# Output-gate projection of the mLSTM mixer in 16 pieces between the steps of its head loop, gate by tanh

## The reference

```python
def mlstm_mixer(h, w_in, conv_w, conv_b, gate_b, head_gain, w_out):
    z = h @ w_in                        # columns: q and k (raw), v, o, gates
    ...
    h_fwd = mlstm_chunkwise(q, k, v, g[0, 0], log_sigmoid(g[0, 1]))      # 8 heads, chunks of 128 tokens
    h_bwd = flip(mlstm_chunkwise(flip(q), flip(k), flip(v), ...))
    hs = (h_fwd + h_bwd).transpose(0, 2, 1, 3)
    hs = rms_norm(hs) * head_gain       # over the 128 columns of each head; eps = 1e-6
    out = jax.nn.sigmoid(o).reshape(...) * hs
    return out.reshape(B, S, 1024) @ w_out
```

## Time and profile before

| what | value |
|---|---|
| three runs | 2610.43, 2621.83, 2626.52 us; median 2621.83 |
| profiled execution | 2625.2 us; its span, from first to last instruction, 2623.4 us |
| mean granted TensorE clock over the span | 0.961 |
| TensorE busy | 2515.0 us, 96% of the span |
| VectorE, ScalarE, GpSimd busy | 1237.9, 907.2, 66.6 us (47%, 35%, 3%) |
| instructions | 30460 |

### The profile page before, as it was taken

The page is one execution under the profiler, slowest core; times in us unless marked ns, Lnnn a source line. Parts: engine busy times, 40 slices in busy tenths (PEclk is TensorE's granted clock), DMA queues, the critical chain, the costliest instruction groups (busy, mean ns, idle before and its releaser), DMA issues.

```text
span 2623.4 us, 30460 instructions
## 1 busy us (share of the span) xinstructions
PE 2515.0 (96%) x12342; PEld 2076.9 (79%) x12342; DVE 1237.9 (47%) x1476; ACT 907.2 (35%) x1221; POOL 66.6 (3%) x80
## 2 busy tenths in 40 slices
PE   7989999999998999999999999999988999999998
PEld 6657888888996678888878888799856977788886
DVE  6678533357624553332254441546585623544423
ACT  3453333213424333332243331334444434433311
POOL 0300000000002000000000000000000000000000
PEclk9999999998996699999999999999988999999999
DMA  8135522472222022222222222231100330222221
GB/s 339 52 119 199 186 89 96 176 272 80 99 69 95 21 80 98 96 96 96 92 84 96 96 96 96 79 111 65 65 17 17 121 120 33 80 96 96 96 96 64
DMA packets 40407, 267.36 MB, mean 102 GB/s; under 512 B 4378, under 2 KB 5658, under 8 KB 9218
## 3 DMA queue, kind: packets, MB, share of 16 engines
q1 hardware_dynamic: 31248, 219.87, 23.4%
q0 software_dynamic: 5696, 40.37, 4.0%
q10 hardware_dynamic: 3378, 5.91, 0.7%
HBM read 263.90 MB, written 2.24 MB: 101 GB/s over the span
## 4 chain that ended last, share of the span: by engine, by line
PE 85%; DVE 8%; ACT 4%; issue 1%; DMA 1%; ACTq 0%; SPq 0%; DVEq 0%
PE bank L222 24%; PE bank L223 24%; PE bank L224 24%; PE bank L1852 2%; ACT w_hi L205 1%; DVE w_lo L209 1%; PE bank L1850 1%; PE bank L325 1%; DMA work<-stream 1%; PE bank L2132 1%; PE bank L2215 1%; PE bank L253 1%; PE bank L254 1%; PE bank L259 1%; DVE work L449 1%
## 5 line engine op out<-in xcount | busy, mean ns | idle before, releaser
L222 PE MATMUL bank<-h_hi,w_hi 128*128 128x512 f32 x1880 | 740.9, 394 | 7.4 <-DVE h_lo L564 2.3
L224 PE MATMUL bank<-h_hi,w_lo 128*128 128x512 f32 x1880 | 735.1, 391 | 0.0
L223 PE MATMUL bank<-h_lo,w_hi 128*128 128x512 f32 x1880 | 734.7, 391 | 0.0
L209 DVE TENSOR_TENSOR w_lo<-raw,w_hi 128x2048 fp32r<-128x2048 f32 x192 | 440.9, 2296 | 602.0 <-ACT w_hi L205 602.0
L205 ACT ACTIVATE w_hi<-raw 128x2048 fp32r<-128x2048 f32 x192 | 366.4, 1908 | 425.9 <-PE bank L224 417.2
L222 PEld LDWEIGHTS bank<-h_hi,w_hi 128*128 128x128 f32 x1880 | 355.0, 189 | 87.7 <-issue 8.4
L224 PEld LDWEIGHTS bank<-h_hi,w_lo 128*128 128x128 f32 x1880 | 354.8, 189 | 75.2
L223 PEld LDWEIGHTS bank<-h_lo,w_hi 128*128 128x128 f32 x1880 | 355.2, 189 | 72.7 <-issue 0.5
L222 PE MATMUL bank<-g_hi,w_hi 128*128 (+1 forms) x704 | 279.1, 396 | 0.0
L223 PE MATMUL bank<-g_lo,w_hi 128*128 (+1 forms) x704 | 279.1, 396 | 0.0
L224 PE MATMUL bank<-g_hi,w_lo 128*128 (+1 forms) x704 | 279.1, 396 | 0.0
(11 more groups left out here) (290 smaller groups left out, 2772.9 us busy)
## 6 DMA issues: line engine op xcount, KB each, us to landing
raw<-stream SPq DMA_DIRECT2D x192, 1024.0 KB, 4.8
work<-stream POOLq DMA_DIRECT2D x19, 1024.0 KB, 6.9
h_plain<-stream POOLq DMA_DIRECT2D x16, 1024.0 KB, 5.4
work<-stream SPq DMA_DIRECT2D x13, 1024.0 KB, 12.5
work<-mlstm_rows ACTq DMA_DIRECT2D x8, 512.0 KB, 4.7
x<-xT SPq DMA_DIRECT2D x1, 2048.0 KB, 9.3
outT<-work SPq DMA_DIRECT2D x8, 256.0 KB, 2.3
work<-mlstm_rows ACTq DMA_DIRECT2D x8, 192.0 KB
```

The source lines that it names most:

```text
L209: nc.vector.tensor_tensor(w_lo[:, slot(m), :], raw[:, slot(m), :], w_hi[:, slot(m), :], ALU.subtract).then_inc(lo_split, 1)
L222: nc.tensor.matmul(out, stationary[0], moving[0], start=first, stop=False)
L223: nc.tensor.matmul(out, stationary[0], moving[1], start=False, stop=False)
L224: return nc.tensor.matmul(out, stationary[1], moving[0], start=False, stop=last)
```

## The change

1. Units 9 to 12 leave the row of units. Right after unit 8 TensorE makes all eight carried states.
2. The work of units 9 to 12 is cut into 16 pieces (`piece`), each one block of 128 tokens of one unit: 8 x 3 = 24 products of 256 columns. Piece r is put ahead of the sums of step r-1, two of them ahead of step 0. The pieces write banks 0 and 1, two pieces to a bank.
3. With banks 2 and 3 alone left, `score` makes one head at a time, at every odd step: 4 products (8 instructions) on one half of the rows.
4. ScalarE evacuates two pieces at a time with `tanh(x / 2)` (`take_gate`, 8 instructions of 128 x 512) in place of four sigmoids of 128 x 1024, and no longer changes its table between exponentials and gate. `gate_rows` becomes `(tanh + 1) * rows`, which is twice the sigmoid's product; the factor of two is taken back in the roots (`scale=4/group`, `bias=4 eps`).
5. The split of units 11 to 14 of the stream (counted from this stage's first) moves into the head loop: high parts behind every second `take_gate`, low parts on VectorE at steps 4, 8, 12 and 16.
6. `scale_keys` and the first transfer of queries are made one or several units earlier; buffers in SBUF are moved so that these can live beside each other.

Cut to its core:

```diff
@@ scalar
-                for u in range(13):
+                for u in range(9):
-                    if u == 12:
-                        self.exps(act, st, 0)
-                        self.exps(act, st, 1)
-                        act.wait_ge(self.s_moved, 48)
-                        self.load_queries(act, 1)
-                        nc.scalar.activation(self.o[:, :, c:c + 256], two_banks(m), ACT.Sigmoid).then_inc(self.s_evac, 1)
+                self.exps(act, st, 0)
+                for i in range(8):
+                    self.copy_state(act, i)
+                self.exps(act, st, 1)
+                act.wait_ge(self.s_moved, 48)
+                self.load_queries(act, 1)
                 for q in range(2, 2 * self.H):
+                    if d == 0:
+                        self.take_gate(act, h - 1)
                     self.exps(act, st, q)
...
+            def take_gate(self, act, g):
+                m, c = self.m0 + 9 + g // 2, 256 * (g // 2)
+                if g % 2:
+                    act.wait_ge(unit_used, m + 1)
+                else:
+                    act.wait_ge(self.s_pe_prep, 15 + g // 2)
+                nc.scalar.activation(self.o[:, 2 * (g % 2):2 * (g % 2) + 2, c:c + 256],
+                                     bank[:, g % 2, :].rearrange("p (t n) -> p t n", t=2), ACT.Tanh,
+                                     scale=0.5).then_inc(self.s_evac, 1)
+                if g % 2:
+                    split_next_hi(act, m)
@@ vector
-                    if u == 8:
+                    if u == 7:
                         self.scale_keys(dve)
-                    if q >= 4 and q % 2 == 0:
-                        self.tail.gate_rows(dve, q // 2 - 2)
-                self.tail.gate_rows(dve, self.H - 1)
+                    if q % 4 == 0 and q:
+                        split_next_lo(dve, self.m0 + 8 + q // 4)
+                    if q >= 6 and q % 4 in (2, 3):
+                        self.gate(dve, 2 * (q // 4) - 4 + q % 4)
+                for h in (self.H - 2, self.H - 1):
+                    self.gate(dve, h)
                 self.tail.vector(dve, st)
@@ tensor
-                    if u in (9, 10):
-                        pe.wait_ge(self.s_keys, 12)
-                        pe.wait_ge(self.s_evac, 9)
-                        for p in range(4):
-                            self.add_state(pe, u - 9, p)
-                pe.wait_ge(self.s_copied, 8)
+                pe.wait_ge(self.s_keys, 12)
+                pe.wait_ge(self.s_evac, 9)
+                for d in range(2):
+                    for p in range(4):
+                        self.add_state(pe, d, p)
+                pieces = 0
                 self.score(pe, 0)
                 for q in range(2 * self.H):
-                    if q % 4 == 2 and q < 14:
-                        self.score(pe, (q + 2) // 4)
+                    if q % 2 and q < 15:
+                        self.score(pe, (q + 1) // 2)
+                    while pieces < min(q + 2, 16):
+                        self.piece(pe, pieces)
+                        pieces += 1
+                    if q == 0:
+                        pe.wait_ge(self.s_copied, 8)
                     self.sum_values(pe, q)
...
+            def piece(self, pe, r):
+                m, t, g = self.m0 + 9 + r // 4, r % 4, r // 2
+                wh, wl = unit_cols(m)
+                if t == 0:
+                    pe.wait_ge(lo_split, m + 1)
+                if r % 2 == 0 and g >= 2:
+                    pe.wait_ge(self.s_evac, 8 + g)
+                c = slice(t * P, t * P + P)
+                for k in range(KC):
+                    last = three_passes(bank[:, g % 2, (r % 2) * 256:(r % 2) * 256 + 256], (h_hi[:, k, c], h_lo[:, k, c]),
+                                        (wh[:, k, :], wl[:, k, :]), k == 0, k == KC - 1)
```

More of the change, by code:

```diff
@@ L59 @@
           ("hg_gnorm", 4), ("sb_gnorm", 4), ("gate_b_i", 1), ("gate_b_f", 1), ("eps", 1), ("zero", 1),
-          ("one", 1), ("half", 1)]
+          ("one", 1), ("half", 1), ("eps4", 1)]
 PCOL = {}
@@ L908, in take_roots @@
                 act.wait_ge(self.sq, self.groups)
-                nc.scalar.activation(self.roots, self.sums, ACT.Sqrt, bias=eps, scale=1.0 / self.group).then_inc(
-                    self.root, 1)
+                four = 4.0 if self.gate_tanh else 1.0
+                nc.scalar.activation(self.roots, self.sums, ACT.Sqrt, bias=col("eps4") if self.gate_tanh else eps,
+                                     scale=four / self.group).then_inc(self.root, 1)
             def gate_rows(self, dve, b):
@@ L914, in gate_rows @@
                 c = slice(b * P, b * P + P)
+                if self.gate_tanh:
+                    nc.vector.scalar_tensor_tensor(self.rows[:, :, c], self.gate[:, :, c], 1.0, self.rows[:, :, c],
+                                                   ALU.add, ALU.mult).then_inc(self.gated, 1)
+                    return
                 nc.vector.tensor_tensor(self.rows[:, :, c], self.rows[:, :, c], self.gate[:, :, c],
@@ L1451, in program @@
             rows_out = area(21056, S + 3 * P)
-            e, se = area(16448, 2, S), area(17472, 2, S)
-            qs = [area(18496 + 768 * a, 2, 3 * P) for a in range(2)]
+            e = [area(19520, S), area(16448, S)]
+            se = area(18496, 2, S)
+            qs = [area(a, 2, 3 * P) for a in (3328, 16960, 17728, 16960)]
             c = [area(20032 + 387 * a, 3, P + 1) for a in range(8)]
@@ L1678, in vector, with gate @@
                         self.scale_queries(dve, (q + 2) // 4)
[L1679 to L1681 removed]
+                    if q % 4 == 0 and q:
[4 more added lines that the diff above has]
+                    self.gate(dve, h)
                 self.tail.vector(dve, st)
+            def gate(self, dve, h):
+                dve.wait_ge(self.s_evac, 9 + 2 * (h // 2) + 2)
+                self.tail.gate_rows(dve, h)
             def factors(self, st):
@@ L1820, in add_state, with score @@
                 last.then_inc(self.s_pe_prep, 1)
[L1822 to L1829, removed]
+            def piece(self, pe, r):
[9 more added lines that the diff above has]
+                                        (wh[:, k, :], wl[:, k, :]), k == 0, k == KC - 1)
+                if t == 1:
+                    last.then_inc(self.s_pe_prep, 1)
+                if t == 3:
+                    last.then_inc(unit_used, 1)
+            def score(self, pe, h):
+                if h >= 2:
+                    pe.wait_ge(self.s_se, 2 * h - 2)
+                half = slice(64 * (h % 2), 64 * (h % 2) + 64)
                 for a in range(TB):
                     t = slice(a * P, a * P + P)
[L1832 to L1835, removed]
+                    last = nc.tensor.matmul(bank[:, 2 + h % 2, t], self.qk[half, 4 + h // 2, t], self.qk[half, h // 2, t],
+                                            start=True, stop=True)
                 last.then_inc(self.s_scored, 1)
@@ L2671, in build_params @@
             columns(i["final_norm_2"]), columns(i["hg_lb_raw_2"]), columns(i["hg_gnorm_2"]), columns(i["sb_gnorm_2"]),
-            gb, np.full((P, 1), EPS, f), np.zeros((P, 1), f), np.ones((P, 1), f), np.full((P, 1), 0.5, f)]
+            gb, np.full((P, 1), EPS, f), np.zeros((P, 1), f), np.ones((P, 1), f), np.full((P, 1), 0.5, f),
+            np.full((P, 1), 4 * EPS, f)]
     out = np.ascontiguousarray(np.concatenate(cols, axis=1))
```

31 lines of the change are left out of this document (14 added, 17 removed).

## The result

The changed kernel took 2579.85 us (median of four, 2578.01 to 2582.02) against 2623.98 us for the kernel before in the same comparison. The ratio is 0.9842, with a 95% interval of 0.9807 to 0.9878: 1.6% faster. The forecast was 2611.7 us with a range of 2588 to 2632, so the result lies outside it. It is 5.8 us from the first rival, in which the clock holds (2585.6 us).

What follows compares the result with a forecast made beforehand. TensorE at half clock was taken to bound the head loop. The loop was to end 11.3 us earlier (full-clock gain 37.4, less 26 for falls), the tail to cost 1.2: -10.1 us from 2621.8, so 2611.7 us, range 2588 to 2632.

Steps and rivals of the forecast that it cites:

- The bound: Head loop: bound by TensorE, busy for 81.5 of 81.7 us at a clock of 0.52.
- which clock: New head loop: clock falls in plain stretches and returns with pieces; ten falls of 5.2 us lose 26 us.
- Full clock holds: Rival, head loop: pieces keep TensorE at 1.00, gain 36.2 us, 2585.6 us; chance 0.15.
- Half clock rules: Rival: pieces too short to restore the clock, nearly all the loop at 0.50, 42.2 us slower, 2664 us; chance 0.05.
- A new wait in the loop: Rival: gates, splits and scores late by a microsecond a step, 16 us lost, 2628 us; chance 0.10.
- Start and states: Ahead of the loop: 1.3 us idle for unit 8's values, then eight states in 11.0 us at full clock.
- Pieces, sums, scores: Head loop at full clock: pieces 46.1 us, sums 46.7, scores 8.0, changes of kind 3.2.
- ScalarE, VectorE, queues: Head loop: their added gates, splits and possible table loads are covered; tanh and exponentials probably need no load between them.
- Tail: Step 16 and after: VectorE's split and both last gates stand in a row, costing 1.2 us.
- within 1%: Whole kernel: time between 2595.6 and 2648 us, no change that runs can tell; chance 0.77.

Runs made afterwards that it cites:

- the one without its long wait: The kernel before, with VectorE's last low split moved behind the first two weighings; 2611.7 us.
- all pieces ahead: The changed kernel with all 16 pieces made after the first scores and ahead of the first sums; 2594.8 us.
- both kernels with the last pieces behind: The changed kernel with the last two pieces behind the last sums, 2578.9 us; the same with pieces also two at a time ahead of even steps, 2571.1 us.
- the light one: The changed kernel with all pieces ahead of the first sums and most of VectorE's products with queries and gates left out; 2576.5 us.
- Thin pieces: The changed kernel with one pass of three in the pieces, 2548.8 us; with 24 extra ScalarE copies making a gap ahead of the first sums, 2562.5 us.
- pairs: The changed kernel with pieces made two at a time ahead of every even step, none ahead of odd ones; 2574.6 us.
- order: The changed kernel with scores at odd steps put behind the piece, right ahead of the sums; 2572.5 us.

## Why the prediction was wrong

**The bound.** Right. The loop was TensorE's, at half clock, and what it was worth hung on the clock. I put both prices in the sum, and the result came out at the one for full clock.

**The step that failed** is "which clock", the term of 26 us. It rested on a reading of the loop's one stretch at full clock: "once granted full clock, they lost it after 3.3 us". The row itself says that TensorE was busy for 3.02 of those 3.30 us. The missing 0.28 us is a wait, and the clock fell 0.4 us behind it:

```profile
839.50 0.49 PE L1852 MATMUL bank<-work 128*128 128x129 f32 x2
840.27 0.46 PE L1850 MATMUL bank<-work 64*128 64x129 f32 x2 [0.28 <-DVE work L1727]
840.65 0.80 PE L1852 MATMUL bank<-work 128*128 128x129 f32 x2
```

I took for a property of the work what came with a wait. The runs put in its place: sums and scores alone kept full clock for 24 us until a wait of 0.24 us, and for a whole loop of 48.5 us where nothing made TensorE wait; they lost it at waits of 0.24 to 4.1 us; at half clock they stayed there for 44 us. Of the ten falls that I had put into the loop, there was none. That a wait is the cause, and does not only go with the fall, is shown for the one of 4.1 us, which was put in. For those below 1 us it is not shown: six falls in five traces (the kernel before, the one without its long wait, all pieces ahead, and both kernels with the last pieces behind) came 0.4 to 2.3 us behind a wait of 0.24 to 0.96 us. In the second model, waits of 0.38 and 0.46 us between plain products cost no clock over 20 us (the last of the earlier trace rows).

Nor does every fall need a wait. Earlier in the changed kernel TensorE makes 32 products of one column in a row. The profile shows it busy throughout, and the clock fell in their midst, at 354.1 us:

```profile
351.57 4.55 PE L325 MATMUL bank<-tab,work 128*128 128x1 f32 x32
355.99 0.77 PE L222 MATMUL bank<-h_hi,w_hi 128*128 128x512 f32 x1
```

So what the runs above say of waits holds for these sums and scores, and a stretch of thinner work can lose the clock by itself, as I had supposed of the sums.

**The rivals.** "Full clock holds" was what happened, and had a chance of 0.15. Its argument, pieces that keep TensorE at 1.00, is only half of why. The pieces' other service is the greater one in a loop entered at full clock: with 2.9 us of work between one sums and the next, VectorE's chain is never late, so there is no wait to lose the clock by. With the pieces ahead of the loop, in step 7 it was late by 0.24 us, and the kernel took 18.3 us more than the light one that had no wait. Thin pieces of 1 us were enough cover too: that loop has no wait. Beyond that they bring the clock back after a gap. The rule that I cited beside this rival, from the Trainium skill (TensorE: Matmul & The Clock Gate, What's actually happening), gave the right side here and in the light kernel. The 44 us at 100% busy and half clock contradict it still, and such stretches of 44 us and more stand in four kernels now; so does the fall in the midst of the products of one column. As the profile counts busy, it is not enough to raise the clock, nor always to keep it. "Half clock rules" lost by the same runs: after a real gap the pieces brought the clock back in 12 us, and thin ones in 17. "A new wait in the loop" had nothing to it; there was none.

**Start and states.** 1.4 us of wait against 1.3, 10.7 us of states against 11.0. The copies of states and the first weighing were hidden as said.

**Pieces, sums, scores.** Pieces took 48.0 us against 46.1 + 3.2, scores 8.7 against 8.0. Sums were mis-sized: I took 7 x 0.417 = 2.92 for all, but they measure 2.82 us at even steps and 2.55 at odd ones, where two products of one kind stand next to each other and their parts start 0.11 us apart in place of 0.21. That makes 43.2 us in place of 46.7, and with the other terms, 0.9 us less together, the loop ended at 843.6 in place of 848.0. Taking out 6 of the 11.6 us of waits was worth 10.3 us by experiment, of 44.

**ScalarE, VectorE, queues.** Hidden, all of them, and exponentials and tanh needed no load between them. The tanh takes 0.58 us; its avoided loads would have been hidden too.

**Tail.** I had +1.2 us for the split in the tail. The wait ahead of the transposes grew from 5.3 to 6.2 us, 0.9. The chain that ended last has the split where I put it:

```profile
844.54 0.86 DVE work L1775 x3
845.40 1.79 DVE w_lo L209
...
848.11 0.68 DVE work L918
848.80 0.27 DVE small L926
849.10 0.70 DVE work L935
849.84 1.13 PE bank L967 x4
```

**The chances.** With 0.77 on "within 1%" I trusted an estimate of alternation that no row had shown; the trace had both clocks for both kinds of work, and its one fall inside the loop could be read two ways. The two ends, 2586 and 2664, should have carried more of the chance between them, and the range should have reached the nearer one.

## What to carry to other kernels

Where TensorE runs gapless at half clock, look for the wait, or the thinner work, that came before the stretch, since work behind it can take almost twice as long for as long as it is sparse; and read a short busy stretch for the gap inside it before drawing a law from it. Putting independent dense work into a loop that has to wait for other engines can pay twice: it covers the waits, and it brings the clock back when one gets through. And when products on half of the rows are made, put those of the other half next to them: the swap of two calls gained 4.3 us of the loop here.

## What the hardware showed beyond this

The plain 4-byte products of 129 columns tended to stay at the clock that they found: at 0.42 us a product they held 1.00, at 0.73 us they held 0.50, and one wait of about a quarter of a microsecond was all that lay between the two in one run (24 us at full clock before it, 44 us at half behind it). The clock came back without pieces in two traces, behind the scores of two heads at once, for 3.4 us each. Products on one half of the rows ran among those on the other half even when they came from different loops of the code (L1876 and L1892 above). Two edits that each changed nothing in the amount of work, pairs (2574.6 us) and order (2572.5 us), did about as well as anything tried that keeps the whole computation (2571.1 us).
